# The preparation of a scan runs under the projection and the attention ahead of it

## The reference

```python
def even_mixer(u_ctx, u_lat, w_in, w_out, a_prm, sink, rope_ang, need_ctx):
    p_ctx = u_ctx @ w_in
    p_lat = u_lat @ w_in
    a_lat, a_ctx = rwkv7_mixer(p_ctx[..., :A_IN], p_lat[..., :A_IN], a_prm, need_ctx)
    ...
    b_lat = banded_window_attention(ql, kl, vl, kc, vc, sink_g)
    b_ctx = context_attention(qc, kc, vc, sink_g)

def rwkv7_prepare(pa, prm):
    ...
    w_raw = prm['w0'] + jnp.einsum('bsdl,dlc->bsdc', jnp.tanh(wl), prm['w2'])
    decay = jnp.exp(-jnp.exp(-jax.nn.softplus(-w_raw) - 0.5))
    iclr = jax.nn.sigmoid(prm['a0'] + jnp.einsum('bsdl,dlc->bsdc', al, prm['a2']))
    kk = (k * prm['k_k']).reshape(bn, s, A_HEADS, HEAD_DIM)
    kk = kk / jnp.maximum(jnp.sqrt(jnp.sum(kk * kk, axis=-1, keepdims=True)), 1e-12)
    k_dir = k[:, :, None, :] * (1 + (iclr - 1) * prm['k_a'])

def rwkv7_scan(f, d, s0, reverse):
    def step(state, inp):
        r_t, w_t, k_t, v_t, kk_t, a_t = inp
        sa = jnp.einsum('bhvk,bhk->bhv', state, -kk_t)
        state = (state * w_t[:, :, None, :] + sa[..., None] * (kk_t * a_t)[:, :, None, :]
                 + v_t[..., None] * k_t[:, :, None, :])
        return state, jnp.einsum('bhvk,bhk->bhv', state, r_t)
```

## Time and profile before

| what | value |
|---|---|
| median of 3 runs | 2146.01 us (2144.9 to 2160.28) |
| the profiled run | 2151.01 us, its span 2149.2 us |
| PE busy | 1962.7 us, 91% of the span |
| DVE busy | 1138.1 us, 53% |
| ACT busy | 871.9 us, 41% |
| POOL busy | 229.1 us, 11% |
| mean granted clock of PE | 0.947 of full speed |

### The profile page before, as it was taken

The page is one execution under the profiler, slowest core; times in us unless marked ns, Lnnn a source line. Parts: engine busy times, 40 slices in busy tenths (PEclk is TensorE's granted clock), DMA queues, the critical chain, the costliest instruction groups (busy, mean ns, idle before and its releaser), DMA issues. The chain is left out here.

```text
span 2149.2 us, 36826 instructions
## 1 busy us (share of the span) xinstructions
PE 1962.7 (91%) x15695; PEld 1632.8 (76%) x15695; DVE 1138.1 (53%) x1790; ACT 871.9 (41%) x1540; POOL 229.1 (11%) x257
## 2 busy tenths in 40 slices
PE   5997999899799999998699988989999979888998
PEld 4756998675699888765588876878888758667986
DVE  4555675455577564345555655354444545535643
ACT  4344564435465542363222224232222244545542
POOL 1100121110022200002211222020000011000000
PEclk9987999999799999997699999989999989998999
DMA  7573665458366542360700022433222204104553
GB/s 248 177 275 117 177 178 188 145 180 311 96 188 185 186 125 73 102 222 18 26 4 4 4 93 86 94 84 98 98 88 89 98 21 148 49 20 132 183 193 120
DMA packets 237754, 264.54 MB, mean 123 GB/s; under 512 B 20374, under 2 KB 159894, under 8 KB 237207
## 3 DMA queue, kind: packets, MB, share of 16 engines
q1 hardware_dynamic: 228167, 259.23, 39.2%
q10 hardware_dynamic: 9424, 2.95, 0.8%
HBM read 261.07 MB, written 1.09 MB: 122 GB/s over the span
## 5 line engine op out<-in xcount | busy, mean ns | idle before, releaser
L401 PE MATMUL acc<-rounded,rounded 128*128 128x512 f32 (+1 forms) x2552 | 882.0, 346 | 39.3 <-DVE rounded L648 11.0
L402 PE MATMUL acc<-rounded,rounded 128*128 128x512 f32 (+1 forms) x2552 | 876.7, 344 | 0.0
L403 PE MATMUL acc<-rounded,rounded 128*128 128x512 f32 (+1 forms) x2552 | 875.5, 343 | 0.0
L385 DVE TENSOR_TENSOR rounded<-arena,rounded 128x2048 fp32r<-128x2048 f32 x194 | 435.0, 2246 | 307.9 <-ACT rounded L374 307.8
L401 PEld LDWEIGHTS acc<-rounded,rounded 128*128 128x128 f32 x2552 | 488.7, 192 | 106.4 <-issue 32.0
L402 PEld LDWEIGHTS acc<-rounded,rounded 128*128 128x128 f32 x2552 | 489.1, 192 | 60.1 <-issue 0.2
L403 PEld LDWEIGHTS acc<-rounded,rounded 128*128 128x128 f32 x2552 | 488.2, 191 | 61.2
L374 ACT ACTIVATE rounded<-arena 128x2048 fp32r<-128x2048 f32 x194 | 362.9, 1873 | 360.7 <-PE acc L403 332.6
L1914 PE MATMUL sc<-arena 64*64 64x64 f32 x2560 | 101.7, 228 | 23.8 <-DVE arena L2044 12.4
L1914 PEld LDWEIGHTS sc<-arena 64*64 64x64 f32 x2560 | 89.5, 141 | 34.1 <-DVE arena L2044 15.7
L1388 DVE SCALAR_TENSOR_TENSOR arena<-acc,pcol,arena 128x254 f32<-128x254 f32 (+1 forms) x176 | 76.8, 478 | 52.4 <-ACT arena L1369 50.8
(11 more groups left out here) (238 smaller groups left out, 1769.8 us busy)
## 6 DMA issues: line engine op xcount, KB each, us to landing
arena<-in_w_ff SPq DMA_DIRECT2D x64, 1024.0 KB, 5.3
arena<-in_w_ada SPq DMA_DIRECT2D x48, 1024.0 KB, 5.1
arena<-in_w_up SPq DMA_DIRECT2D x88, 512.0 KB, 5.0
arena<-in_w_in SPq DMA_DIRECT2D x24, 1024.0 KB, 5.1
arena<-in_w_down SPq DMA_DIRECT2D x20, 1024.0 KB, 5.0
arena<-in_w_out SPq DMA_DIRECT2D x16, 1024.0 KB, 5.0
arena<-in_w_in_even SPq DMA_DIRECT2D x9, 1024.0 KB, 5.2
arena<-in_w_in_odd SPq DMA_DIRECT2D x8, 1024.0 KB, 5.1
```

The source lines that it names most:

```text
L385: dve.tensor_tensor(r32(w), w, r32(high_slot(c)[:, 0:size(c)]), ALU.subtract).then_inc(split_made, 1)
L401: pe.matmul(ps, ah, bh, start=first, stop=False)
L402: pe.matmul(ps, ah, bl, start=False, stop=False)
L403: return pe.matmul(ps, al, bh, start=False, stop=last)
```

## The change

The preparation is taken out of the place between attention and scan, and its pieces are written into the lists of the stages before.

- `projB` is split in two: keys and values first (`projB_kv`), then queries (`projB_q`) in the order 2, 3, 0, 1. Squares are made by ACT within `projA`. The sums by head stand on PE in the second half of `projB_kv`. In the first half of `projB_q` four low-rank products stand before each token tile, in the second half the two key transposes of a tile. The sigmoids write straight into the arrays of the running sums and rates; the running sums run in place on DVE before the query rotations. Attention starts when the two latent query tiles are turned.
- Under latent attention DVE makes the decays in units 0 and 1 and one `kd` in each of units 2 to 9, and the widened norm in unit 8.
- Under context attention PE turns the widened norm in units 0 to 3 and the values in units 4 to 7, DVE multiplies the norm in, ACT keeps the values, POOL makes `kka`.
- After attention only the two context tiles of the output are turned; the latent ones and `ada_gains` stand in the first scan step. SP no longer waits for `prep_done` and `kka_done` ahead of the gate writes, so `mod_ready` alone holds them.
- The buffers are laid out anew, the bonus sum of the scan is written into the other direction's key, and its second half is made one step earlier.

```diff
-        stage("projB", acc=8, tr=8)
-        plan_tok("projB", I["w_in_even_2"][0][:, A_IN:A_IN + 768], KT, acc_at["projB"], [ALL] * 2)
+        stage("projB", acc=8)
+        plan_tok("projB_kv", I["w_in_even_2"][0][:, A_IN + 512:A_IN + 768], KT, acc_at["projB"], [ALL])
+        plan_tok("projB_q", I["w_in_even_2"][0][:, A_IN:A_IN + 512], KT, acc_at["projB"] + 4, [ALL])
+        stage("kk_sum", sc=1)
+        for j in range(4):
+            stage(("prep", j), sc=2, tr=2)
+        stage("kT", tr=4)
+        stage("qT", tr=4)
...
-        stage("attBc", acc=16, tr=8 + 4, sc=8 + 4)
+        stage("attBc", acc=16, tr=8 + 4 + 8, sc=8 + 4)
...
-        stage("kk", acc=1, tr=4)
-        stage("prep", acc=16)
-        stage("v_turned", tr=NCH // 2)
...
+                    for i in range(2):
+                        for d in range(2):
+                            s = slice(d * 64, d * 64 + 64)
+                            ps = claim(pe, "tr" if i else "sc", lora_fill(i, n, d))
+                            pe.matmul(ps[:, :], lora[s, i, n * P:(n + 1) * P], pA[s, 12 + i, :], start=True, stop=True)\
+                              .then_inc(tr_full if i else sc_full, 1)
...
+                    wait_drained(pe, "acc", acc_at["projB"] + n)
+                    if n >= TT:
+                        pe.wait_ge(roped, n - TT + 1)
+                    ps = claim(pe, "tr", tr_at["kT"] + n)
+                    for j in range(2):
+                        ins = pe.transpose(ps[:, j * P:(j + 1) * P], k_tok[:, n, j * P:(j + 1) * P], ident)
+                    ins.then_inc(tr_full, 1)
...
+            tok_gemm(pe, "projB_kv", acc_at["projB"], KT, [ALL], token_tile, before=sums)
+            tok_gemm(pe, "projB_q", acc_at["projB"] + 4, KT, [QUERIES], token_tile, before=among)
...
+            for n, tt in enumerate(QUERIES):
+                wait_drained(pe, "acc", acc_at["projB"] + 4 + n)
+                if tt >= TT:
+                    pe.wait_ge(roped, tt + 1)
...
+            edge = const("scan_edge")
+            for j in range(4):
+                for d in range(2):
+                    wait_drained(dve, "sc", lora_fill(0, j, d))
+                    x = lc[d][:, j, :]
+                    if d == 0:
+                        dve.tensor_tensor_scan(x, edge[:, 0:S2], x, 0.0, ALU.mult, ALU.add).then_inc(summed, 1)
+                    else:
+                        dve.tensor_tensor_scan(x[:, ::-1], edge[:, 1:S2 + 1][:, ::-1], x[:, ::-1], 0.0, ALU.mult, ALU.add).then_inc(summed, 1)
+            for tt in range(TT):
+                wait_drained(dve, "acc", acc_at["projB"] + 4 + tt)
+                rope(dve, q_tok(TT + tt), 8, tt, rope_t, roped, TT + tt + 1)
+            dve.wait_ge(acc_full, acc_at["projB"] + 8)
+            for j in range(4):
+                dve.tensor_scalar(kk[:, j, :], kf[:, j, :], col("a_k_k_2", j), None, ALU.mult).then_inc(kk_done, 1)
...
+        def kd_dve(dve, d, j):
+            t = rope_t[:, j % 2, :]
+            wait_drained(dve, "tr", lora_fill(1, j, d))
+            if d and j == 0:
+                dve.wait_ge(kk_done, 4)
+            link(dve, dve.scalar_tensor_tensor(t, rates[d][:, j, :], -1.0, kf[:, j, :], ALU.add, ALU.mult))
+            dve.scalar_tensor_tensor(kd[d][:, j, :], t, col("a_k_a_2", j), kf[:, j, :], ALU.mult, ALU.add).then_inc(prep_done, 1)
+        def under_latent_dve(dve):
+            def hook(u):
+                if u < 2:
+                    decays_dve(dve, u)
+                else:
+                    kd_dve(dve, *divmod(u - 2, 4))
+                if u == 8:
+                    dve.wait_ge(kk_rn, 1)
+                    dve.tensor_copy(kk_wide.rearrange("p j (b e) -> p (j b) e", e=HD), kk_rs[:, :].unsqueeze(2).broadcast_to([P, 32, HD]))                       .then_inc(kk_widened, 1)
+            return hook
...
+        def under_context_pe(pe, att):
+            def hook(u):
+                ps = claim(pe, "tr", att.more[u])
+                if u < 4:
+                    pe.wait_ge(kk_widened, 1)
+                    wide = kk_wide.rearrange("p j t -> p (j t)")
+                    for tt in ALL:
+                        c = 8 * tt + 2 * u
+                        ins = pe.transpose(ps[:, tt * P:(tt + 1) * P], wide[:, c * HD:(c + 2) * HD], ident)
+                else:
+                    for c in range(2):
+                        i = 2 * (u - 4) + c
+                        chunk = vf[:, :, i * CH:(i + 1) * CH]
+                        for j in range(4):
+                            for h in HEADS:
+                                ins = pe.matmul(ps[h, (4 * c + j) * CH:(4 * c + j + 1) * CH], chunk[h, j, :], eye64[h, :], start=True, stop=True)
...
+            def hook(u):
+                i = u - 5
+                if i >= 0:
+                    if i == 0:
+                        act.wait_ge(prep_done, 8)
+                    f = att.more[4 + i]
+                    act.activation(v_turned[:, 2 * i:2 * i + 2, :, :].rearrange("p c j v -> p (c j v)"), filled(act, "tr", f)[:, :],
+                                   ACT.Copy).then_inc(drain("tr", f), 1)
...
+                j = u - 1
+                if 0 <= j < 4:
+                    ps = filled(dve, "tr", att.more[j])
+                    if j == 0:
+                        dve.wait_ge(kk_done, 4)
+                    dve.tensor_tensor(kk[:, j, :], kk[:, j, :], ps[:, :], ALU.mult).then_inc(drain("tr", att.more[j]), 1)
...
+        def prep_pool(pool, att):
+            pool.wait_ge(prep_done, 8)
             for d in range(2):
-                step_exps(act, d, 0)
-                act.activation(f_step[d], l_step[d], ACT.Exp, scale=-DECAY).then_inc(decay_ready, 1)
-        def prep_pool(pool):
-            for j in (2, 3):
-                wait_drained(pool, "tr", tr_at["kk"] + j)
-            for m in range(8):
-                d, j = divmod(m, 4)
-                wait_drained(pool, "acc", prep_fill(d, j, 1))
-                pool.tensor_tensor(kka[d][:, j, :], kk[:, j, :], iclr[:, j % 2, :], ALU.mult).then_inc(kka_done, 1)
+                for j in range(4):
+                    wait_drained(pool, "tr", att.more[3 if d else j])
+                    pool.tensor_tensor(kka[d][:, j, :], kk[:, j, :], rates[d][:, j, :], ALU.mult).then_inc(kka_done, 1)
...
+            act.wait_ge(kka_done, 8)
+            act.wait_ge(prep_done, 8)
+            for d in range(2):
+                step_exps(act, d, 0)
+                act.activation(f_step[d], l_step[d], ACT.Exp, scale=-DECAY).then_inc(decay_ready, 1)
...
+            if first_step:
+                yTB_turn(pe, *LATS)
...
+            if s == 0:
+                yTB_dve(dve, LATS)
+                ada_gains(dve, att_bc, 1)
...
-                    sp.wait_ge(prep_done, 8)
-                    sp.wait_ge(kka_done, 8)
                     sp.wait_ge(mod_ready, 2 * DEPTH)
                     for post in posts.values():
...
+            att_bl.vector(dve, under_latent_dve(dve))
+            att_bc.vector(dve, under_context_dve(dve, att_bc))
             for d in range(2):
                 step_ar(dve, d, 0)
+            yTB_dve(dve, LAT)
...
```

354 lines of the change are left out of this document (156 added, 198 removed).

## The result

| | before | changed |
|---|---|---|
| median, us | 2149.53 (4 runs, 2144.9 to 2160.28) | 2118.32 (4 runs, 2115.32 to 2123.59) |
| ratio to before | 1 | 0.9855, 95% interval 0.9834 to 0.9876 |
| profiled execution, us | 2151.0 (span 2149.2) | 2123.59 (span 2121.7) |

The kernel became 31 us faster, 1.45%. Predicted were 2112 us, from a sum of 33.8 us off; 2118 lies in the range (2098 to 2128). Of the 6.1 us between forecast and median, 3.5 come from the kernel before, whose median over four runs is 2149.5 and was 2146.0 over the three that the forecast started from; 2.6 are the gain itself, 31.2 us where 33.8 were said. The profiled execution of the changed kernel is the slowest of its four, so the two spans differ by 27.5 us only.

The account below looks back on a forecast made before the run. PE, busy 91% of 2149.2 us, was taken as the bound, except in the chain between attention and scan. Terms of -57.3, +9.7, +4.4, +7.6 and +1.8 gave 33.8 us off: 2112 us from the median of 2146.0, range 2098 to 2128.

Parts of the forecast that it names:

- A: Between the last turned attention block and PE's first scan matmul: 61.3 us shrink to 4.0, 57.3 us off.
- B: Second projection and its tail: norm sums, low-rank products and key transposes added on PE, tail shorter; 9.7 us on.
- C: Start of latent attention: two decay blocks on DVE delay the first units, 4.4 us on; key-direction pairs cost nothing.
- D: Context attention: delayed first maxima, 16 transposes of the widened norm and 64 matmuls for turned values; 7.6 us on.
- E: First scan step: 3.0 for gate writes, 0.5 for latent transposes, less 1.7 for first products; 1.8 us on.
- 3 us more of it than before: First scan step: gate writes moved behind the gains put the 20 us jam wholly where PE is dense; 3 us on.
- the unpaired products: Rival, second projection: low-rank pairs don't overlap, 6.9 us more, 2119 us; chance 0.12.
- the attention bound by DVE: Rival, attention: key-direction pairs on DVE are all exposed, 11.5 us more, 2124 us; chance 0.13.
- the free jam: Rival, first scan step: gate writes cost nothing since PE has its instruction blocks, 17 us less, 2095 us; chance 0.08.
- The jam at double cost: Rival, first scan step: gate writes moved to the densest place cost double, 12 us more, 2124 us; chance 0.07.
- a wait on issue of 10 us or more: Expected sign in the first or second scan step, with gate writes issued about 7 us after its start.
- a first step over 50 us: Sign that the prediction is wrong: the first scan step taking over 50 us.

Follow-up runs that it names:

- experiment 8: Changed kernel with each group of four low-rank products taken from one half of the rows; ratio 0.9869 to the kernel before.
- experiment 1: Changed kernel with the gates turned on PE and written by one DMA in rows of 512 bytes; median 2098.96 us, ratio 0.9757 to the kernel before.
- experiment 2: Changed kernel with the six element-by-element gate writes held until the fourth scan step has begun; ratio 0.9889 to the kernel before.
- experiment 4: Kernel before with only the gates turned on PE and written in rows of 512 bytes; ratio 0.993 to the kernel before.
- Experiment 3: Changed kernel with the second layer's gains made ahead of the scan's first factors, so gate writes go out earlier; ratio 0.9866 to the kernel before.
- gates_split: Changed kernel with the first layer's four gate writes issued under the second projection, two left in the first scan step; ratio 0.9801 to the kernel before.
- lora_unpaired: Changed kernel with each group of four low-rank products ordered by row half instead of alternating; ratio 0.9863 to the kernel before.

## Why the prediction was right, and where it was not

| term, us | predicted | measured in the two profiles |
|---|---|---|
| A, gap between attention and scan | -57.3 | (1003.66 - 999.09) - (1040.85 - 979.56) = 4.57 - 61.29 = -56.7 |
| B, second projection and its tail | +9.7 | (914.26 - 863.16) - (905.20 - 863.50) = 51.10 - 41.70 = +9.4 |
| C, latent attention | +4.4 | (964.88 - 914.26) - (951.25 - 905.20) = 50.62 - 46.05 = +4.6 |
| D, context attention | +7.6 | (999.09 - 964.88) - (979.56 - 951.25) = 34.21 - 28.31 = +5.9 |
| E, first scan step | +1.8 | 51.13 - 44.09 = +7.0 |
| rest of the span | 0 | -0.3 ahead of it, +2.7 behind it |

- **A** held to 0.6 us. The chain that must stand between, exponentials, two POOL products and PE's start, is what is left of the gap.
- **B** held, and its chosen end (pairs at 1.06 us against 15.4 us for all sixteen) has its proof in experiment 8. The key norm sums took 3.8 us (predicted 4.0), the eight pairs 4 x 1.92 = 7.7 us (predicted 8.5), and the tail shrank by 3.5 us (predicted 3.8). By the Trainium skill ("TensorE: Matmul & The Clock Gate", Part 3) products in different row groups run together; the trace agrees, with starts 6 to 7 ns apart, 0.96 us for a pair and, in experiment 8, 0.91 us for one alone.
- **C** held in its sum, with errors inside that cancel. A decay block takes 3.1 us on DVE here, not the 4.0 read off. The row that differs is its third, a copy of 32 columns: 1.13 us there, beside a POOL product that runs from 1021.23 to 1023.40 and ends with it, and 0.20 us here, where POOL does nothing. So DVE has the combine of unit 1 ready 14.8 us behind the first score, 1.7 earlier than laid out; but PE, at half clock behind its wait of 2.94 us, has adaptive products, scores and values ahead of that turn and comes to it at 16.35. The slack behind the key-direction pairs was 0.76 us a unit, predicted 0.6. (The units' pace is 5.0 us in both kernels, not the 5.3 that the prediction called the old one.)
- **D** was 1.7 us too dear. The delay of the first maxima is there (0.9 us, predicted 1.0), and so are the turns of the widened norm. But one of the four groups of turned values does not lie in D: it stands on PE behind the last attention turn, 1.1 us beside the chain of A, where the prediction too had put it, and so was counted twice. The remaining 0.6 us were not traced.

```profile
997.79 0.60 PE L810 MATMUL tr<-keep,arena 128*128 128x128 f32 x4
998.33 1.15 PE L1824 MATMUL tr<-keep,arena 64*64 64x64 f32 x32
```

- **E is the step that failed**, in size. That a jam exists, that it costs some 14 us before, that it moves behind the gains into the dense part of the step: all shown (experiments 1, 2, 4). The term "3 us more of it than before" was worked out from where 20 us of jam lie over idle time. That shift itself was right: the packets of the six writes run for 23.7 us before, from 3.7 us ahead of the scan's first matmul, and for 22.7 us now, all behind it. But the jam grew by more than the shift: by 20.9 - 12.8 = 8.1 us in the two pairs of profiles, by some 6 in the whole times, so the term should have been 5 to 8 within the spread of these readings. The first products and the latent turns together did save what was said: 31.25 against 30.23 us for the step without the jam, 1.0 where 1.7 - 0.5 = 1.2 was predicted. Experiment 3 put the writes back ahead of the scan and got 0.5 us. So it seems not to be the place relative to the scan's first matmul alone. Its writes still went out 3.1 us later against the scan's first matmul than those of the kernel before, and met first products at full clock. Which of these two makes the jam cheaper in the kernel before stays open. A rough view of it was in reach: the earlier trace rows shows the writes 4.6 us ahead of a first product that waits 5.3 us for POOL and then takes 5.49 us, 10 us in which PE takes few instructions. That cover is gone in the changed kernel; that it is the cause is not shown.
- **The rest**: from the second scan step to the end are 1066.9 us, before 1064.3. In the profiles of the experiments in which nothing behind that point differs it is 1066.3 to 1071.5, in gates_split 1061.9. That part varies by more than the 2.7 us from one execution to another, and nothing is read into it. Together with the 0.3 us ahead of the projection it is what separates the sum of the terms (29.8 us off) from the 27.5 us of the spans; the medians are 31.2 apart. That the sum of the terms came within 4 us of the predicted one is in part luck: E's miss of 5.2 us was offset by D's 1.7.

Of the rivals, the unpaired products, the attention bound by DVE and the free jam did not come. The last one is the Trainium skill's case ("Runtime: NRT & Kernel Launch", Instruction fetch mechanics, where refill is mostly hidden): here the trace does not agree, since the jam costs 25.0 us in an otherwise quiet scan step. The jam at double cost was half right: its mechanism, the densest place, came with 5 us of the 12.

The text of the prediction spoke of a wait on issue of 10 us or more in one of the first steps. There is none: the longest wait of the changed kernel's first step is 5.22 us, the others are 0.2 to 2.4, and a third of the loss is the lower clock between them (experiment 1). Its other mark, "a first step over 50 us" as a sign of an error, did turn up, at 51.13, and pointed at the right term.

## What to carry to other kernels

When work moves, ask what the idle time that it fills was hiding: here the first scan step, with a jam of element-by-element writes in it, became 7 us longer when the gap in front of it was gone, though what in the gap had made the jam cheaper is open. A store whose inner element is one number is to be judged by what it does to the engines that take many instructions, not by its bytes; turning 64 columns once on PE (0.4 us) and writing rows made 21 us, and if that is not possible, put such writes together under wide matmuls (four of them cost under 1 us there), not spread over the dense steps. After pulling a chain forward, look again at each engine's idle stretch upstream: DVE had 11 us free that took the two decay blocks and gave 4.6 us back.

## What was not expected of the hardware

- Six writes of 4 KB, element by element, cost a dense scan step 25.0 us, two 9 us (38.57 against 29.7), one 4.2 to 6.7 us. The same values as one 32 KB write of 512-byte rows, with the 1 MB load behind it, cost at most 0.6 us (27.03 against 26.44). Under 512-column matmuls four of them cost at most 0.9 us.
- A single such write takes 1.4% of the DMA engines' time in its step, and still the next block of instructions takes 3.74 us instead of about 1.2, the one after starts 9.1 us behind it, and PE waits 4.04 us on issue. Beside six writes a block takes 9.61 us.
- Behind such a wait PE's granted clock is lower (0.50 to 0.54 from 1110 to 1116.5, behind the wait of 4.04 us; 0.90 over the step, against 1.00), and six writes one by one cost 38.5 us where six at once cost 19 to 25.
- Two 64-row products of different halves ran together though a product of the first half stood between them in the kernel's text (14 ns between their starts, in lora_unpaired). Whether the compiler or the engine reordered them was not tried.
- A DVE copy of 32 columns took 1.13 us beside a POOL product and 0.20 us with POOL idle; the block around it 4.0 and 3.1 us. The two rows before the change:

```profile
1021.23 2.17 POOL L1778 TENSOR_TENSOR arena<-arena 128x512 f32<-128x512 f32 x1 [1.93 <-ACT arena L1761]
1022.32 1.13 DVE L1804 COPY stat<-arena 128x32 f32<-128x32 f32 x1
```
